# Convolution taps of all items but the first: from VectorE to products on ScalarE and sums on TensorE

## What is computed

```python
def mixer(h, hist_pool, hist_dw, hist_sc, ...):
    p = h @ w_in                                  # 1024 -> 2176
    u_pool, c_val, c_gate, s_h, s_b, s_c = jnp.split(p, cuts, axis=-1)
    y_a, nh_pool = pool_mixer(u_pool, ...)
    z = c_val * jax.nn.sigmoid(c_gate)            # 384 channels
    zc, nh_dw = causal_depthwise(z, hist_dw, w_dw)   # width 31, one filter per channel
    y_b = jax.nn.silu(layer_norm(zc + b_dw, ln_g, ln_b))
    ys, nh_sc = causal_depthwise(s_c * s_h, hist_sc, w_sc)   # width 3
    return jnp.concatenate([y_a, y_b, s_b * ys], axis=-1) @ w_out, ...

def peer(h, w_q, sub_keys, expert_u, expert_v):   # 16384 experts per layer
    # 8 heads: scores of two half keys, top 16 of each, top 16 of their sums -> 128 ids a token
    act = gelu(jnp.einsum('td,thkd->thk', xb, expert_u[idb]))
    return jnp.einsum('thk,thkd->td', gtb * act, expert_v[idb])
```

## Time and profile before

| | us |
|---|---|
| median of the runs | 3323.06 |
| the profiled execution | 3350.05 |
| its span, from first to last instruction | 3348.3 |
| VectorE busy | 2166.2 |
| GpSimd busy | 2070.0 |
| TensorE busy | 1997.2 |
| ScalarE busy | 306.7 |

### The profile page before, as it was taken

How to read it: one execution, slowest core, us unless ns; L and a number is a source line. 1 busy time by engine, 2 the same in 40 slices (tenths; PEclk the granted TensorE clock), 3 DMA queues, 4 the chain that set the end, 5 groups by cost and what they waited for, 6 DMA issues and landing times.

```text
span 3348.3 us, 23981 instructions
## 1 busy us (share of the span) xinstructions
PE 1997.2 (60%) x7260; PEld 667.8 (20%) x7260; DVE 2166.2 (65%) x5654; ACT 306.7 (9%) x657; POOL 2070.0 (62%) x2196
## 2 busy tenths in 40 slices
PE   8355756456634564678845356447784537454498
PEld 6112212111211121112212112111231212111122
DVE  4868588758878767635387967764619797636500
ACT  3100111101010001000101000000010010000000
POOL 1566665666665656566665656666666565666665
PEclk9668888778877876789977687678997768776699
DMA  6799998999999999999998989999999998999998
GB/s 248 285 365 339 368 353 336 373 365 370 373 365 342 359 385 403 409 406 362 361 374 307 388 327 378 364 354 374 363 354 363 341 359 332 374 370 383 380 375 327
DMA packets 333869, 1201.37 MB, mean 359 GB/s; under 512 B 41511, under 2 KB 41897, under 8 KB 331692
## 3 DMA queue, kind: packets, MB, share of 16 engines
q0 software_dynamic: 313344, 1140.99, 89.7%
q1 hardware_dynamic: 19164, 49.42, 4.0%
q10 hardware_dynamic: 1232, 9.44, 0.7%
HBM read 1188.82 MB, written 10.87 MB: 358 GB/s over the span
## 4 chain that ended last, share of the span: by engine, by line
POOL 26%; DVE 21%; another core or an unknown queue 17%; issue 17%; PE 13%; DMA 5%; ACT 2%; DVEq 0%; ACTq 0%; POOLq 0%
POOL rows L711 26%; DVE rows L1754 8%; PE acc L1230 7%; DVE psB L1427 4%; DMA rows<-in_expert_u,ids 3%; DMA rows<-in_expert_v,idsT 2%; DVE work L1515 1%; PE psB L1163 1%; PE psA L1076 1%; DVE work L1508 1%; DVE work L1505 1%; DVE work L1549 1%; DVE work L1555 1%; DVE work L1561 1%
## 5 line engine op out<-in xcount | busy, mean ns | idle before, releaser
L1230 PE MATMUL acc<-rows,strip 128*32 128x512 f32 x4352 | 1162.5, 690 | 586.4 <-DMA rows<-in_expert_v,idsT 390.5
L1754 DVE CUSTOM_DVE_ANT_0 rows<-rows,psH 128x1024 f32<-128x1024 f32 x1088 | 1287.5, 1218 | 343.4 <-DMA rows<-in_expert_u,ids 204.9
L711 POOL DMA_INDIRECT rows<-in_expert_v,idsT x1088 | 1030.9, 948 | 613.6 <-issue 273.0
L711 POOL DMA_INDIRECT rows<-in_expert_u,ids x1088 | 1023.9, 941 | 611.2 <-issue 313.9
L1230 PEld LDWEIGHTS acc<-rows,strip 128*32 128x32 f32 x4352 | 225.5, 117 | 1425.7 <-issue 714.5
L1427 DVE SCALAR_TENSOR_TENSOR psB<-zbuf,chan,psB 128x128 f32<-128x128 f32 (+1 forms) x827 | 203.4, 329 | 26.9 <-DVE psB L1427 21.9
L1019 PE MATMUL psA<-w_out_sb,hT 128*128 128x512 f32 x288 | 165.9, 725 | 73.8 <-issue 58.4
L1059 PE MATMUL psB<-w_in_sb,hT 128*128 128x512 f32 x288 | 156.0, 696 | 59.9 <-DVE hT L1408 34.6
L1163 PE MATMUL psB<-w_q_sb,hT 128*128 128x512 f32 x288 | 150.8, 673 | 62.5 <-issue 35.8
L1761 DVE TENSOR_TENSOR x_out<-acc,x_out 128x1024 f32<-128x1024 f32 x10 | 12.2, 1222 | 245.5 <-PE acc L1230 201.5
L1076 PE MATMUL psA<-w_in_sb,hT 128*128 128x512 f32 x288 | 138.7, 635 | 1.7 <-DVEq L1595 1.7
(11 more groups left out here) (227 smaller groups left out, 1412.8 us busy)
## 6 DMA issues: line engine op xcount, KB each, us to landing
rows<-in_expert_u,ids POOLq DMA_INDIRECT x1088
rows<-in_expert_v,idsT POOLq DMA_INDIRECT x1088
w_in_sb<-in_w_in SPq DMA_DIRECT2D x4, 2176.0 KB, 30.2
w_out_sb<-in_w_out SPq DMA_DIRECT2D x2, 4096.0 KB, 18.4
w_q_sb<-in_w_q SPq DMA_DIRECT2D x2, 4096.0 KB, 24.7
w_in_sb<-in_w_in ACTq DMA_DIRECT2D x2, 2176.0 KB, 22.7
x_mid<-x_mix SPq DMA_DIRECT2D x8, 512.0 KB
w_in_sb<-in_w_in ACTq DMA_DIRECT2D x1, 3264.0 KB
```

The costliest lines, as they stand in the source:

```text
L711: nc.gpsimd.indirect_dma_start(out=rows[:, j, :], out_offset=None, in_=table[:, :], in_offset=bass.IndirectOffsetOnAxis(ap=index, axis=0))\
L1230: last = nc.tensor.matmul(acc[LS * g:LS * (g + 1), c:e], strip[:, first:first + LS], rows[:, at % RING, c:e], start=start, stop=stop, skip ...
L1754: nc.vector.tensor_tensor_reduce(rows[:, j, :], rows[:, j, :], psH[:, :], 1.0, 0.0, ALU.mult, ALU.add, dots[:, r:r + 1]).then_inc(s_free[j ...
```

## The change

The taps of all items but the first leave VectorE. ScalarE makes each of the 93 products z shifted by k times tap (the bias comes in with tap 0) into one of five buffers of 128 x 128: the three chunks of `zc`, `best`, and a piece of `work`. TensorE adds each product into `p_conv` with a matmul by the identity. Semaphores count products made (`s_tp`) and products added (`s_ts`); product i waits until product i - 5 has been added. TensorE has a `yield` before each four of these matmuls. In tick 11 ScalarE copies the sums to `zc` (`keep_conv`), and MEAN waits for that too. VectorE's `taps` now does nothing for these items, nor yields. `U_LONG` gets weights of 5 in ticks 8 to 11, where it had 0, and smaller ones elsewhere, so expert_u rows are fetched and dotted in those ticks too. In n = 1 one `keep_quarter` on ScalarE comes after the mixer's part of its tick.

```diff
+SHARED = 3
+PIECE = 4
-U_LONG = [0, 6, 6, 7, 7, 8, 7, 8, 0, 0, 0, 0, 1, 6, 6] + [5] * 9 + [7, 7] + [0] * 16
+U_LONG = [0, 5, 5, 6, 6, 6, 6, 6, 5, 5, 5, 5, 4, 4, 4] + [4] * 9 + [6, 6] + [0] * 16
...
+        products = [zc[:, c, :] for c in range(SHARED)] + [best[:, :], work[:, 1216:1216 + P]]
+
+        def shared_taps(m, tick):
+            first = SHARED * (HC + 1) * (m - 1)
+            return [(first + SHARED * k + c, k, c) for k in taps_of(tick) for c in range(SHARED)]
...  ScalarE
+            def tap_products(m, tick):
+                l, L = layer(m), width(m)
+                if tick == CONV:
+                    act.wait_ge(s_z, m + 1)
+                for i, k, c in shared_taps(m, tick):
+                    if i >= len(products):
+                        act.wait_ge(s_ts, i - len(products) + 1)
+                    to, z, w = products[i % len(products)][:, 0:L], zbuf[:, c, k:k + L], chan[:, l, c, k:k + 1]
+                    if k == 0:
+                        nc.scalar.activation(to, z, ACT.Identity, bias=chan[:, l, c, BIAS:BIAS + 1], scale=w)\
+                            .then_inc(s_tp, 1)
+                    else:
+                        nc.scalar.activation(to, z, ACT.Copy, scale=w).then_inc(s_tp, 1)
+
+            def keep_conv(m):
+                L = width(m)
+                act.wait_ge(s_ts, SHARED * (HC + 1) * m)
+                nc.scalar.copy(zc[:, 0:SHARED, 0:L], p_conv[:, 0:SHARED, 0:L]).then_inc(s_zk, 1)
...
+                if m and CONV <= tick < CONV + CONV_TICKS:
+                    tap_products(m, tick)
                 if tick == KEEP_B and m:
...
                     act.sem_inc(s_yp, 1)
+                    if m:
+                        keep_conv(m)
...
                         gelu_of(n, part)
-                        keep_quarter(n, part)
+                        if (n, tick) != (1, GELU_AT[1][0]):
+                            keep_quarter(n, part)
...
                         mixer(n + 1, tick)
+                    if (n, tick) == (1, GELU_AT[1][0]):
+                        keep_quarter(1, 0)
...  TensorE, after PROJ_C and before TURN_B
+                if m and CONV <= tick < CONV + CONV_TICKS:
+                    for at, (i, k, c) in enumerate(shared_taps(m, tick)):
+                        if at % PIECE == 0 and (at or tick == CONV):
+                            yield
+                        pe.wait_ge(s_tp, i + 1)
+                        nc.tensor.matmul(p_conv[:, c, 0:L], ident[:, :], products[i % len(products)][:, 0:L],
+                                         start=k == 0 and c == 0, stop=k == HC, skip_group_check=True).then_inc(s_ts, 1)
...  MEAN
+                    if m:
+                        pe.wait_ge(s_zk, m)
...  VectorE
-                chunks = CC if m else CC - 1
-                for k in some:
-                    if k % 3 == 2:
+                own = range(SHARED, CC) if m else range(CC - 1)
+                chunks = len(own)
+                for k in some if own else ():
+                    if m or k % 3 == 2:
                         yield
-                    for c in range(chunks):
+                    for c in own:
```

More of the change, by code:

```diff
@@ L448, in build @@
         s_zc = sem("conv_done")
+        s_tp = sem("tap_products_made")
+        s_ts = sem("tap_products_added")
+        s_zk = sem("conv_sums_copied")
         s_mean = sem("ln_sum")
```

## The result

| kernel | median us | range, runs | ratio to before, 95% interval |
|---|---|---|---|
| before | 3328.77 | 3322.06 to 3334.56, 4 | |
| after | 3472.82 | 3467.86 to 3494.42, 4 | 1.0446 [1.0395, 1.0497] |

The change makes the kernel 4.5% slower, 144 us. The prediction was 3301 us with a range up to 3362 and 0.22 for slower: wrong in sign, and outside the range. (The median of before here is over four runs, the 3323.06 above over the first three.) The profiled execution of after took 3473.81 us (span 3471.9), 123.8 more than that of before.

What follows compares the result with a forecast made beforehand. The prediction took the DMA stream of expert row fetches as the bound. From the profiled 3350.05 us it took 30 for VectorE's relief, added 8 for TensorE's adds, and scaled 3328.05 by 0.992 to 3301 us; range 3248 to 3362.

Steps and rivals of the forecast that it cites:

- Row stream as the bound: Whole kernel: indirect row fetches set the time; an engine costs time only where occupied ring slots let the DMA queue run dry.
- VectorE's relief: Nine convolution stages and stretches behind two of them: taps leaving VectorE lets the row stream run faster, gaining 30 us.
- VectorE's busy time: Sign to check: VectorE's total work falls from 2166 to some 1965 us.
- Rows moved: Ticks 8 to 11 of six stretches get 22 expert_u rows from other ticks; same number of fetches, so 0 us.
- ScalarE's products: 93 products an item, 28.4 to 36.2 us on ScalarE, mostly beside TensorE's rows; no term in the sum.
- rival B: Ticks 8 to 11 of m = 1, 2, 5, 8: taps pace TensorE, 51 us lost, 3358 us; chance 0.25.
- TensorE's adds: 93 identity matmuls an item, 22.7 us, hidden except in stages m = 1, 2, 5, 8; cost 8 us.
- The ring's cover: 13 fetch slots, 19 us of stream, let TensorE fall 11 us behind in each of four stages before a slot is missing.
- my own 41: TensorE's excess over stage length at m = 1, 2, 5, 8, together 41 us before allowing for the fetch slots.
- The hand-off: Products from ScalarE to TensorE: with 5 buffers ScalarE runs five ahead, mostly beside TensorE's rows; waits given no separate term.
- sign to watch for: Sign of the slower outcome: GpSimd's idle behind TensorE well over 111 us, with four stages 10 us or more longer.

Runs made afterwards that it cites:

- the kernel with four items: Kernel after with products and adds only in items 3, 4, 6 and 9, one expert_v row after each 3 taps: 3050.19 us, 1.0011 on chip 3047.

## Why the prediction was wrong

- *Row stream as the bound: right*, but misread. The stream is where the loss is paid; GpSimd's wait for TensorE rose by 223 us while its unresolved waits fell by 96. The prediction took those unresolved waits (398.7 us) as no engine's. By the count of the slot, 349.6 us of them stand before fetches into a slot that a TensorE row had emptied, and that had ended long before (see the section on the hardware). With them, the waits for slots emptied by TensorE are 461 us in before, not 111.3, and 612 us in after.
- *VectorE's relief, 30 us (bounds 16 to 53): too large.* Measured 11 (0.9967). The sign that it was small stood in the earlier trace rows: only 90.7 us of GpSimd's idle was behind dots, and that number is the same after the taps have gone. The forecast of VectorE's busy time was good (1965 us, measured 1960.7); what it is worth was not. I read the lost rate of the convolution stages as VectorE's, because VectorE was the busy engine in them.
- *Rows moved, 0: right* in before (1.0012); with the taps on TensorE they seem to help by about 1%.
- *ScalarE's products, 0: nearly right* as work, 3 to 13 us. The duration was right too: median 386 ns and two in 0.69 us in the rows above, so the wait in front of each product doesn't destroy the overlap; nor is the pace of 0.389 a product, which rival B used, what happened.
- *TensorE's adds, 8 us: the term that failed as a size.* Alone they cost 49 us net of the relief on chip 3356. The 0.244 us an add was a burst's price, and right for one. In after the line holds 304.2 us, 0.36 an add, and 137 us of idle in front. The ring's cover, which took 44 of rival B's 95 us and most of my own 41, was not there: with 24 taps a tick, rows taken in fours between the first taps and 16 to 20 taps in a row behind them, TensorE was behind the stream for a whole stage and its aftermath. The four stretches lose 95 us. The cover counted 13 slots as free when their rows end; where a fetch waits unresolved for a slot of TensorE, the update comes a median of 10 us after that, about as much as the whole cover. That this is what used it up was not tested.
- *The hand-off: the step that failed as a mechanism.* "With the 5 buffers ScalarE runs five products ahead, so most of it lies beside TensorE's rows" gave the new waits no price of their own. They are 99 of the 162 us on chip 3356, and 19 of the 22 on chip 3047. Five buffers are 1.5 us of ScalarE's work; one late update of 0.7 to 2 us empties that reserve, and after it both engines go at the pace of the updates.
- *Rival B was right in place and sign* ("Place: ticks 8 to 11 of m = 1, 2, 5 and 8") and in its sign to watch for, GpSimd's idle behind TensorE well over 111 us. Its size was too small: 3358 us, 35 above before, against 144 measured. It had the pace of products but no price for a wait, and it subtracted a cover. Without that subtraction it gives (3350 - 16 + 95) x 0.992 = 3402 us, still 71 short. A chance of 0.25 for it was too low, since B asked for only one thing, that TensorE be late in stages in which it already was busy for 57 to 73%.

## What to carry to other kernels

A small ring between two engines that hand over one short piece at a time can cost by the rhythm of its waits, not by the work, as on the slower chips here: ask how many microseconds of work the ring holds, and compare that with the longest unresolved wait in the profile (6.6 us in before, against 1.5 us held here). When a wait is put down to an engine, count which of its instructions had to come first, and look when that one ended and when its update is recorded. Before relieving an engine, remove its work without a replacement, on paper or on the chip: here that gave 11 us as the whole prize. And compare kernels on the same chip: the same two programs were 0.7% apart on one chip and 4.5 to 5% on others.

## What the runs showed of the hardware

The waits that the profile can't resolve ("remote") differ here with the chip, for the same kernel. GpSimd's waits before a fetch in after, on chip 3047:

```profile
  issue: 586.6, 1909
  PE acc L1276: 240.1, 184
  DVE dots L1801: 79.0, 82
  DVEq L1619: 37.3, 1
```

The 302.6 us of "remote" are gone altogether, and the stream runs at 392 GB/s instead of 346. The mean granted clock there was 0.841 against 0.795, but durations are the same (a fetch 937 ns median, a dot 1218 ns mean on both), so it isn't slower engines.

What the "remote" waits were comes out if each fetch is laid beside the row that was in its slot 13 fetches before. Of the 206 in after on chip 3329, 184 (277.0 of 302.6 us) are before a slot that a TensorE row had emptied, and that row's last matmul had ended a median of 10.2 us earlier; 170 of these fetches start 0.26 to 0.33 us after an update of that slot's count is recorded. On chip 3047 all 1088 such updates are recorded within 0.12 us of their matmul's end. So the news from TensorE came late here too.

A like difference stands in VectorE's own chain, with no other engine in it. A tap waits for the tap two or three before it, by a semaphore of VectorE itself. What ended its idle before taps, on chip 3329 (827 and 27 taps, before with the moved rows), and on chip 3047 (479 and 15 taps, the kernel with four items):

```profile
  DVE psB L1427: 20.9, 38
  issue: 10.3, 13
  remote: 7.6, 5
  DVE work L1427: 1.4, 2
```

```profile
  DVE work L1499: 0.3, 2
  DVE work L1509: 0.2, 1
```

40 us in 58 idles against 0.5 us in 3. The Trainium skill (VectorE: DVE Perf Modes, The DRAIN you can't avoid) reports that eight copies took as long with a semaphore after each as with one after the last. No run here takes the semaphores away; with them, the trace of chip 3047 has next to no idle before taps, and on chip 3329 one tap in fifteen waited about 0.7 us more.

It isn't the waiting alone either. TensorE in the run with the adds alone, on chip 3356, where an add waits for nothing:

```profile
2443.11 2.44 PE L1118 MATMUL psB<-ident 128*128 128x128 f32 x18
2446.01 0.49 PE L1118 MATMUL psB<-ident 128*128 128x128 f32 x2 [0.45 <-issue]
2447.42 0.27 PE L1118 MATMUL psB<-ident 128*128 128x128 f32 x1 [0.93 <-issue]
2448.13 0.49 PE L1118 MATMUL psB<-ident 128*128 128x128 f32 x2 [0.44 <-issue]
2449.55 0.27 PE L1118 MATMUL psB<-ident 128*128 128x128 f32 x1 [0.93 <-issue]
```

Nine adds go at 0.27 us each, then one or two records every 0.7 to 1.4 us, with idle even between the two records of one add. Such idle makes 61.7 us before the 1674 records of that line there; in the run with the adds alone and single rows between on chip 3047 it is 0.0. That suggests, and doesn't show, that the adds' 49 us are of the same kind. These stalls have no wait that could end late. Each add raises a semaphore; whether updates that don't get away hold TensorE up, or a late supply of instructions does, stays open, since no run here took the updates away or changed the number of instructions by itself.

Why some chips have late updates stays open as well, and one rival hasn't been tested. On the slower chips a part of the update records is missing from the trace, 33% in after and 40% in before, and on the 3047 chips practically none (1 of 6852 in after). Every time in this document is of an execution that was recorded, so no run tells whether the recording itself has a part in the late updates, and in the difference between the chips.
